# Differential attention: scores from rounded parts, half of each map combined on GpSimd, maps turned three units behind

## The reference

```python
    def attend(qb, kk, vv):
        s = jnp.einsum('bqhmd,bkhmd->bhmqk', qb, kk).astype(jnp.float32) * scale
        p = jax.nn.softmax(s, axis=-1)
        p = p[:, :, 0] - lam_full * p[:, :, 1]
        return jnp.einsum('bhqk,bkhe->bqhe', p.astype(vv.dtype), vv)
```

## Time and profile before

| what | us |
|---|---|
| runs: median (lowest to highest of 3) | 2507.63 (2507.43 to 2507.78) |
| profiled execution: span from first to last instruction (no separate time is given for this execution) | 2508.3 |
| TensorE busy (matmuls) | 2474.0 |
| VectorE busy | 1507.2 |
| ScalarE busy | 990.5 |
| GpSimd busy | 136.8 |
| the attention's 32 units, from the first scores | about 1423.6 to 1550 |

### The profile page before, as it was taken

How to read it: one execution, slowest core, us unless ns; L and a number is a source line. 1 busy time by engine, 2 the same in 40 slices (tenths; PEclk the granted TensorE clock), 3 DMA queues, 4 the chain that set the end, 5 groups by cost and what they waited for, 6 DMA issues and landing times.

```text
span 2508.3 us, 32888 instructions
## 1 busy us (share of the span) xinstructions
PE 2474.0 (99%) x13466; PEld 2067.1 (82%) x13466; DVE 1507.2 (60%) x2618; ACT 990.5 (39%) x1997; POOL 136.8 (5%) x148
## 2 busy tenths in 40 slices
PE   8999999999999999999999999999999999999998
PEld 6878888778888788888888988888888888888887
DVE  8787753555666557766664288676654644633434
ACT  5543242454355442333522377432223423422222
POOL 1000000000010010000122000100000001000001
PEclk9999999999999999999999999999999999999999
DMA  4221012212333144654212100366632222222222
GB/s 148 84 85 35 18 52 87 99 68 70 132 135 120 66 178 175 229 208 151 93 67 85 51 1 15 137 229 227 222 114 86 106 100 91 95 101 101 96 85 72
DMA packets 39944, 270.36 MB, mean 108 GB/s; under 512 B 4337, under 2 KB 4593, under 8 KB 9073
## 3 DMA queue, kind: packets, MB, share of 16 engines
q1 hardware_dynamic: 30064, 206.71, 23.2%
q0 software_dynamic: 9040, 60.33, 6.7%
q10 hardware_dynamic: 688, 1.22, 0.2%
HBM read 266.14 MB, written 2.10 MB: 107 GB/s over the span
## 4 chain that ended last, share of the span: by engine, by line
PE 93%; DVE 4%; ACT 2%; DMA 0%; issue 0%; SPq 0%; DVEq 0%; ACTq 0%
PE bank L142 91%; PE bank L145 2%; DVE w_lo L151 1%; ACT tmp L148 0%; DVE dd L151 0%; DVE x_t L159 0%; DMA w_raw<-in_pack_gates 0%; ACT w_hi L148 0%; DVE tmp L151 0%; DVE change L159 0%; ACT L148 0%; DVE first_lo L159 0%; DVE dd L145 0%; DVE da_stat L168 0%; DVE low L151 0%
## 5 line engine op out<-in xcount | busy, mean ns | idle before, releaser
L142 PE MATMUL bank<-h_hi,w_hi 128*128 128x512 f32 x1824 | 694.5, 395 | 0.1
L142 PE MATMUL bank<-h_lo,w_hi 128*128 128x512 f32 x1824 | 677.1, 390 | 0.0
L151 DVE TENSOR_TENSOR w_lo<-w_raw,w_hi 128x512 fp32r<-128x512 f32 (+3 forms) x746 | 490.2, 712 | 143.5 <-ACT w_hi L148 143.0
L142 PE MATMUL bank<-h_hi,w_lo 128*128 128x512 f32 x1824 | 570.8, 390 | 0.0
L148 ACT ACTIVATE w_hi<-w_raw 128x512 fp32r<-128x512 f32 (+3 forms) x746 | 426.5, 637 | 308.0 <-PE bank L142 293.8
L142 PEld LDWEIGHTS bank<-h_lo,w_hi 128*128 128x128 f32 x1824 | 342.2, 188 | 72.3 <-DVE h_lo L159 0.8
L142 PEld LDWEIGHTS bank<-h_hi,w_hi 128*128 128x128 f32 x1824 | 342.5, 188 | 70.3 <-issue 0.8
L142 PEld LDWEIGHTS bank<-h_hi,w_lo 128*128 128x128 f32 x1824 | 341.5, 188 | 68.1
L142 PE MATMUL bank<-f_hi,w_hi 128*128 128x512 f32 x816 | 315.6, 390 | 0.2 <-DVE w_lo L151 0.2
L142 PE MATMUL bank<-f_lo,w_hi 128*128 128x512 f32 x816 | 300.1, 389 | 0.0
L142 PE MATMUL bank<-f_hi,w_lo 128*128 128x512 f32 x816 | 270.3, 389 | 0.0
(11 more groups left out here) (383 smaller groups left out, 3110.7 us busy)
## 6 DMA issues: line engine op xcount, KB each, us to landing
w_raw<-in_pack_ffn SPq DMA_DIRECT2D x60, 1024.0 KB, 4.8
ada_w<-in_ada_w POOLq DMA_DIRECT2D x48, 1024.0 KB, 5.1
w_raw<-in_pack_mlp SPq DMA_DIRECT2D x32, 1024.0 KB, 4.8
w_raw<-in_pack_gdn_qkv SPq DMA_DIRECT2D x12, 1024.0 KB, 4.7
w_raw<-in_pack_sc_cu SPq DMA_DIRECT2D x8, 1024.0 KB, 4.8
w_raw<-in_pack_ffn SPq DMA_DIRECT2D x8, 768.0 KB, 4.1
w_raw<-in_pack_gdn_z SPq DMA_DIRECT2D x4, 1024.0 KB, 4.7
w_raw<-in_pack_gate_a SPq DMA_DIRECT2D x4, 1024.0 KB, 4.7
```

The lines of the kernel that those rows point to most:

```text
L142: return self.engine.matmul(*a, **k) if self.engine is not None else self
L151: return self.engine.tensor_tensor(*a) if self.engine is not None else self
```

## The change

- **Scores.** `scores(n)` takes the three products of rounded parts: twelve one-pass matmuls in place of four fp32 ones, the maps' halves of the array taking turns. `narrow` is now the third product of the 256 columns of map 0. At the first unit of a head (m == 0) TensorE also waits for GpSimd's `q_lo` of that head.
- **Parts.** GpSimd makes them, four pieces for a head (`parts_of_head`): the rounded keys (copy, 768 columns), the rest of the keys (subtraction, 768), the rounded queries (copy, 512), the rest (512). The rest of the keys lies where `k_all` of the head lay; rounded keys and queries have two tiles each. Heads 0 and 1 are made at the end of `context_pool`, the others one piece behind each of units 2 to 25. `context_made` waits for the last piece of head 1 in place of GpSimd's last rotation.
- **Combination.** VectorE combines columns 384 to 767 only. GpSimd takes columns 0 to 383 in two instructions, the product with the weight and the sum with map 0. Minima, exponentials and the first half of a turn also wait for GpSimd's half.
- **Order.** Maps are turned three units behind the scores in place of two, values four in place of three, the square sums eight in place of seven, and the copy of a finished head comes one step later. `da_diff` and `da_p` keep two tiles.
- **Memory.** `da_stat` and the small norm tiles lie in `rstd`'s place, the rounded queries in `tmp`'s.

```diff
+    def parts_of_head(G, h, piece):
+        i = h % 2
+        if piece == 0:
+            if h < 2:
+                G.wait_ge(*at("dve_da", ("rope", rope_number("q", h))))
+                G.wait_ge(*at("act_da", ("k", h)))
+            else:
+                G.wait_ge(*at("pe_da", ("scores", NCH * (h - 1) - 1)))
+            G.tensor_copy(da_k_hi[i][:, :], k_all[:, h, :]).then_inc(*up("pool_da", ("k_hi", h)))
+        elif piece == 1:
+            G.wait_ge(*at("pool_da", ("k_hi", h)))
+            G.tensor_tensor(da_k_lo[:, h, :], k_all[:, h, :], da_k_hi[i][:, :].bitcast(F32), ALU.subtract).then_inc(
+                *up("pool_da", ("k_lo", h)))
+        elif piece == 2:
+            G.tensor_copy(da_q_hi[i][:, :], da_q[:, h, :]).then_inc(*up("pool_da", ("q_hi", h)))
+        else:
+            G.wait_ge(*at("pool_da", ("q_hi", h)))
+            G.tensor_tensor(da_q_lo[i][:, :], da_q[:, h, :], da_q_hi[i][:, :].bitcast(F32), ALU.subtract).then_inc(
+                *up("pool_da", ("q_lo", h)))
...
         for n in range(DT):
             rope_pool(G, "q", n)
+        for h in range(2):
+            for piece in range(4):
+                parts_of_head(G, h, piece)
...
+            pairs = ((q_hi, k_hi), (q_lo, k_hi), (q_hi, k_lo))
...
             if n >= 2:
                 T_.wait_ge(*at("act_da", ("exp", n - 2, 1)))
-            T_.matmul(place[:, 0, 512:NK], q0, k0[:, 512:NK], start=True, stop=True).then_inc(*up("pe_da", ("narrow", n)))
-            T_.matmul(place[:, 1, 256:NK], q1, k1[:, 256:NK], start=True, stop=True)
-            T_.matmul(place[:, 0, 0:512], q0, k0[:, 0:512], start=True, stop=True)
+            if m == 0:
+                T_.wait_ge(*at("pool_da", ("q_lo", h)))
+            product(0, 0, 512, NK)
+            product(1, 0, 256, NK)
+            product(0, 1, 512, NK)
+            product(1, 1, 256, NK)
+            product(0, 2, 512, NK).then_inc(*up("pe_da", ("narrow", n)))
+            product(0, 0, 0, 512)
+            product(1, 2, 256, NK)
+            product(0, 1, 0, 512)
             T_.wait_ge(*at("pe_da", ("narrow", n)))
-            T_.matmul(place[:, 1, 0:256], q1, k1[:, 0:256], start=True, stop=True).then_inc(*up("pe_da", ("scores", n)))
+            product(1, 0, 0, 256)
+            product(0, 2, 0, 512)
+            product(1, 1, 0, 256)
+            product(1, 2, 0, 256).then_inc(*up("pe_da", ("scores", n)))
...
-            T_.wait_ge(*at("dve_da", ("probs", n)))
+            T_.wait_ge(*at("dve_da", ("probs", n)) if half else at("pool_da", ("probs", n)))
...
-        for n in range(2, len(UNITS)):
-            scores(n)
-            turn(n - 2, 0)
-            if n >= 3:
-                values(n - 3)
-            turn(n - 2, 1)
+        scores(2)
+        for n in range(3, len(UNITS) + 1):
+            if n < len(UNITS):
+                scores(n)
+            turn(n - 3, 0)
+            if n >= 4:
+                values(n - 4)
+            turn(n - 3, 1)
...
                 S.wait_ge(*at("dve_da", ("probs", n - 2)))
+                S.wait_ge(*at("pool_da", ("probs", n - 2)))
...
-                if mp and n >= 2:
-                    turned(n - 2, 1)
-                if mp and n >= 6 and n % 4 == 2:
+                if mp and n >= 3:
+                    turned(n - 3, 1)
+                if mp and n >= 7 and n % 4 == 3:
                     result(n // 4 - 1)
...
-            if 2 <= n < len(UNITS) + 2:
-                turned(n - 2, 0)
+            if n >= 3:
+                turned(n - 3, 0)
...
-            V.scalar_tensor_tensor(d[:, :], p[:, 1, :], s[:, 4:5], p[:, 0, :], ALU.mult, ALU.add).then_inc(
+            right = slice(HALF_KT * P, NK)
+            V.scalar_tensor_tensor(d[:, right], p[:, 1, right], s[:, 4:5], p[:, 0, right], ALU.mult, ALU.add).then_inc(
                 *up("dve_da", ("probs", n)))
...
     def attend_pool(G):
+        def combine(n):
+            s, p, d = da_stat[n % 3], da_p[n % 2], da_diff[n % 2]
+            left = slice(0, HALF_KT * P)
+            if n >= 2:
+                G.wait_ge(*at("pe_da", ("turned", n - 2, 0)))
+            G.wait_ge(*at("dve_da", ("weight", n)))
+            G.tensor_scalar(d[:, left], p[:, 1, left], s[:, 4:5], None, ALU.mult).then_inc(*up("pool_da", ("weighted", n)))
+            G.wait_ge(*at("pool_da", ("weighted", n)))
+            G.tensor_tensor(d[:, left], d[:, left], p[:, 0, left], ALU.add).then_inc(*up("pool_da", ("probs", n)))
+
+        context_made(G)
+        for n in range(len(UNITS)):
+            combine(n)
+            h, piece = divmod(n + 6, NCH)
+            if 2 <= h < DA_H:
+                parts_of_head(G, h, piece)
         residual_pool(G, "da_o", 0, ffn_sum[0])
```

More of the change, by code:

```diff
@@ L287, in build_program @@
     spare_col, two_cols = prm_whole[:, N_PARAMS:N_PARAMS + 1], prm_whole[:, N_PARAMS + 1:N_PARAMS + 9]
+    with ExitStack() as st:
+        da_stat = [sb(st, f"da_stat{i}", [P, 8]) for i in range(3)]
+        da_first, da_sums, da_root = (sb(st, f"da_{n}", [P, DA_H, NCH]) for n in ("first", "sums", "root"))
+        da_gain = sb(st, "da_gain", [P, 1])
     rstd = sb(top, "rstd", [P, T])
+    with ExitStack() as st:
+        da_q_hi, da_q_lo = ([sb(st, f"da_q_{part}{i}", [P, T], F32R) for i in range(2)] for part in ("hi", "lo"))
     tmp = [sb(top, f"tmp{i}", [P, T]) for i in range(4)]
@@ L368, in build_program @@
     with ExitStack() as st:
-        k_all = sb(st, "da_k", [P, DA_H, NK])
+        with ExitStack() as s2:
+            k_all = sb(s2, "da_k", [P, DA_H, NK])
+        da_k_lo = sb(st, "da_k_lo", [P, DA_H, NK], F32R)
         v_all = sb(st, "da_v", [P, KT, D])
@@ L381, in build_program @@
         da_pt = [sb(st, f"da_pt{i}", [P, KT, P]) for i in range(2)]
-        da_stat = [sb(st, f"da_stat{i}", [P, 8]) for i in range(3)]
-        da_first, da_sums, da_root = (sb(st, f"da_{n}", [P, DA_H, NCH]) for n in ("first", "sums", "root"))
-        da_gain = sb(st, "da_gain", [P, 1])
+        da_k_hi = [sb(st, f"da_k_hi{i}", [P, NK], F32R) for i in range(2)]
     with ExitStack() as st:
@@ L3093, in scores, with product @@
             cut, place = slice(m * P, (m + 1) * P), score_banks(n)
[L3094 removed]
+            q_hi, q_lo, k_hi, k_lo = da_q_hi[h % 2][:, cut], da_q_lo[h % 2][:, cut], da_k_hi[h % 2], da_k_lo[:, h, :]
+            pairs = ((q_hi, k_hi), (q_lo, k_hi), (q_hi, k_lo))
+            def product(mp, part, a, b):
+                rows, (q, k) = slice(64 * mp, 64 * mp + 64), pairs[part]
+                return T_.matmul(place[:, mp, a:b], q[rows, :], k[rows, a:b], start=(part == 0), stop=(part == 2))
             if n >= 2:
                 T_.wait_ge(*at("act_da", ("exp", n - 2, 1)))
[L3097 to L3099 removed]
+            if m == 0:
[8 more added lines that the diff above has]
+            product(0, 1, 0, 512)
             T_.wait_ge(*at("pe_da", ("narrow", n)))
[L3101 removed]
+            product(1, 0, 0, 256)
+            product(0, 2, 0, 512)
+            product(1, 1, 0, 256)
+            product(1, 2, 0, 256).then_inc(*up("pe_da", ("scores", n)))
         def turn(n, half):
@@ L3302, in attend_vector @@
                 combine(n - 1)
-            if n >= 7:
-                square_sum(n - 7)
-        for u in range(len(UNITS) - 6, NCH * (DA_H - 1)):
+            if n >= 8:
+                square_sum(n - 8)
+        for u in range(len(UNITS) - 7, NCH * (DA_H - 1)):
             square_sum(u)
```

11 lines of the change are left out of this document (6 added, 5 removed).

## The result

The changed kernel takes **2517.53 us** in the median (2516.26 to 2518.70, 5 runs) where the kernel before takes 2507.63 (2507.43 to 2507.78): ratio 1.0040, 95% interval 1.0029 to 1.0051. It is slower by 9.9 us. The forecast was 2512.1, within 2500 to 2522: the sign was right, but the forecast's 4.5 us of loss are less than half of what was measured, and the range of the likeliest case, 2507.5 to 2517, was missed by 0.5.

What follows compares the result with a forecast made beforehand. Before, a ring over two units bound the attention stage; after, VectorE, held up by GpSimd, at 3.74 us a unit. 29 x (3.74 - 3.627) = +3.3, start and end +1.2: +4.5 on 2507.63 gives 2512.1 us, range 2500 to 2522.

Steps and rivals of the forecast that it cites:

- the likeliest case: Differential attention: GpSimd holds VectorE up, to 3.74 us a unit; 2507.5 to 2517 us, chance 0.45.
- GpSimd's sum: GpSimd's work per attention unit: product 0.70, two-tile sum 0.99, a quarter of a head's four pieces; 3.0 us, under 3.48.
- The interference: VectorE and GpSimd instructions each reading two SBUF tiles run one after the other: mean 0.80 us a unit for VectorE.
- my pattern: GpSimd's product gets in before VectorE's combination, which waits some 0.2; the square sum waits 0.85 behind GpSimd's sum: 1.05 us.
- Rival three: GpSimd is the bound, one-input work as dear as two-input: 4.2 us a unit, 2523.1 us; chance 0.14.
- The forecast's own case: VectorE becomes the bound of the attention stage: 2.95 + 0.80 = 3.74 us a unit, 2512.1 us in all.
- I take 1.08: TensorE's score block per unit: nine times 0.12 us for three one-pass products, 0.31 us less; bounds 1.04 and 2.16.
- the ring: Dependency loop over two units through scores, minimum, exponential, copy and transposes: 7.28 us, 3.64 a unit; 3.48 with new scores.
- rival two: The three-unit lag gives ScalarE's copies air, so TensorE binds at 3.23 us a unit: 2497.3 us; chance 0.13.
- the wait of 0.33: TensorE's weight loads waiting 0.33 us for ScalarE's copy of the transposed map; its vanishing would decide for rival two.
- Rival four: One-pass score products of the array's two halves run in sequence, 2.16 us: 4.03 a unit, 2523.7 us; chance 0.05.
- Start and end: Attention stage: -0.9 us before the first waiting minimum, +2.1 behind the last scores (bounds 0 and 2.8); together +1.2.

Runs made afterwards that it cites:

- Number 5: Changed kernel with GpSimd's product written as a tensor-tensor with the weight column repeated, instead of a tensor-scalar: 2528.86 us, ratio 1.0085 to the kernel before.
- number 7: New scores and parts, VectorE combining whole maps, two-unit lag; parts moved from beside VectorE's combination to under its minimum: 2503.61 us, ratio 0.9985 to the kernel before.
- number 3: Against the kernel before, only turning maps three units behind; fp32 scores, no parts, whole combination on VectorE: 2510.31 us, ratio 1.0010.
- number 10: Against number 7, the last product of the narrow columns issued two products earlier: 2501.48 us, ratio 0.9976 to the kernel before.
- numbers 1: Changed kernel with only the new scores and GpSimd's parts kept; VectorE combines whole maps, lag two units: 2520.2 us, ratio 1.0049 to the kernel before.
- number 4: Changed kernel without the parts of heads 2 to 7, whose scores use the parts of heads 0 and 1: 2507.8 us, ratio 1.0000 to the kernel before.

## Why the prediction was half right

**The step that failed is GpSimd's sum, "3.0 us a unit, under 3.48".** It is 4.01. The one bad term is the product: 0.70 taken, from a range of 0.42 to 0.99. It takes 1.24 alone, above the upper bound, because I took the two-input sum as a ceiling for anything with one input, and the trace of before had no such instruction. My estimate from the Trainium skill, GPSIMD Engine Reference, section 3.1, was 0.58, further off still. Behind VectorE it takes 1.69. That is 1.0 more than forecast: 0.54 by the product's own time, and 0.45 by waiting for VectorE, which the sum left out on this side. The two-input terms held: sum 0.99 against 1.00, key rest 1.89 against 1.83, query rest 1.29 against 1.26. The copies were put too high, 1.3 and 0.9 against 0.83 and 0.61. With pauses of 0.19 a unit this is the 4.01.

**The interference was of the right kind, in the wrong place.** I let the square sum wait 0.54 or 1.05. Of the 20 between 1440 and 1536 us none waits: mean 0.28. GpSimd's tensor-scalar gives way to both instructions of VectorE in this kernel. What waits is the weight (mean 0.62 instead of 0.22) and the combination (0.78 instead of 0.62), for GpSimd's sum and its pieces: 0.56 a unit, where I had 0.80. VectorE needs 2.95 + 0.56 = 3.51 and is not the bound; it waits 10.9 us in 25 units for scores. Number 5 shows my pattern, with 0.66 + 0.81, where the product has two inputs.

**Rival three came true in kind.** GpSimd is the bound, and its condition, a product above 0.85, is met. Its 4.2 a unit was measured as 4.01, and its 2523.1 was 5.6 too high. Its way there was partly another: it had 3.57 of work and 0.6 of waiting; measured are 3.37 of undisturbed work (1.24 + 1.00 + 1.13) and 0.64 of waiting and pauses. I gave it 0.14 where the product had no row at all, which was too little. The forecast's own case, VectorE at 3.74, did not come about; the range held only because it reached most of the way to this rival.

**Scores.** "I take 1.08" was 1.35, inside the bounds: twelve starts, 0.11 to 0.12 apart whether 256 or 512 columns wide. That the new wait on the narrow product costs nothing was wrong by 0.1. The forecast of 3.48 for an undisturbed unit met the measured 3.49 to 3.50 by luck: I had put it on the ring, and it is TensorE's own cycle. So rival two's condition (TensorE full, the wait of 0.33 gone) came true wherever GpSimd was out of the way, with 3.50 in place of its 3.23, and not by the lag it was put on: between 1440 and 1536 us TensorE's loads wait for ScalarE's copy 26 times, 8.6 us, both before and with the lag alone, and never in number 7, which has the old lag. Rival four is out: the halves overlap.

**Start and end.** Forecast -0.9 and +2.1, measured -0.4 and +2.5. The end is the lag's: number 3 shows the same +2.5 with the lag alone, near the 2.15 of one unit's transposes and values. The start gained less because a score block saves 0.14 there (1.25 against 1.39), not 0.31. The lag bought nothing that the runs can show.

**The sum.** Forecast 29 x (3.74 - 3.627) + 1.2 = 4.5; measured 8.2 + 2.1 = 10.3 in the stage.

**Open.** The runs do not say why the tensor-scalar gives way to VectorE while the copies and tensor-tensors do not. They show only which goes first. Two versions were not tried: the changed kernel with its half combination kept and only the parts moved under the minimum, and number 10's scores with a small share on GpSimd.

## What to carry to other kernels

Work for an idle engine is priced from rows of that very form of instruction; where there are none, another form is no ceiling, and the case "this engine becomes the bound" deserves a large chance. Where VectorE and GpSimd share a stage, when each GpSimd instruction starts can matter more than its length: one and the same version lost 12.7 us with its parts beside VectorE's combination, and gained 4.0 with them under a reduction that reads PSUM. Before opening a ring, add up the full engine inside it: in the kernel before, the ring stood at 3.64 and TensorE's own cycle at 1.39 + 2.15 = 3.54.

## What the runs showed of the hardware

- GpSimd's tensor-scalar of 384 columns took 1.24 us undisturbed (1.17 with a constant), the sum of two tiles 1.00, and the same product with a repeated column 0.82. A copy to fp32r took 0.61 for 512 columns and 0.83 for 768.
- Released by the same signal, GpSimd's copies and tensor-tensors started 0.02 to 0.05 us behind VectorE's two-tile instruction and still went first, for their whole length less about 0.17 (numbers 1 and 5).
- The tensor-scalar went second when it started 0.07 behind VectorE's combination, and also when it started 0.02 ahead of it (number 4). When it started 0.10 to 0.30 ahead, it took 1.24 and held the combination up only for its own first 0.37 us.
- A reduction from PSUM on VectorE (1.76 us) ran side by side with GpSimd's copies, subtractions and sums, each at its lone duration (number 7 and the changed kernel).
- One-pass products with half of the rows of the array started 0.11 to 0.12 us apart whatever their width, 256 or 512 columns. Twelve of them, with the two halves taking turns, took 1.25 to 1.35 us, where the four fp32 products they replaced took 1.39.
